# LayerNorm's gain and offset on the residual copy: from GpSimd to VectorE, one quarter in each gate chunk

## What is computed

```python
def layer_norm(x, g, b):
    xf = x.astype(jnp.float32)
    mu = jnp.mean(xf, axis=-1, keepdims=True)
    var = jnp.mean(jnp.square(xf - mu), axis=-1, keepdims=True)
    return ((xf - mu) * lax.rsqrt(var + LN_EPS)).astype(x.dtype) * g + b
...
        x = layer_norm(DEEPNORM_ALPHA * x + y, ln_g[i], ln_b[i])
        x = x + (p[i] @ w_ple[i]) * jax.nn.sigmoid(x @ w_ple_gate[i])
```

## Time and profile before

| | us |
|---|---|
| median of 3 runs | 1190.71 |
| lowest and highest | 1190.23, 1191.17 |
| profiled execution, span from first to last instruction | 1189.1 |
| TensorE busy | 1166.7 |
| VectorE busy | 741.6 |
| ScalarE busy | 589.7 |
| GpSimd busy | 68.4 |

### The profile page before, as it was taken

One profiled execution on the slowest core, in us unless ns is written; L12 is line 12 of the kernel. 1 busy time (PEld: TensorE's weight loads), 2 busy tenths in 40 slices (PEclk: granted clock), 3 DMA queues, 4 the chain that ended last, 5 costly groups with the idle time before them and its releaser, 6 DMA issues.

```text
span 1189.1 us, 15576 instructions
## 1 busy us (share of the span) xinstructions
PE 1166.7 (98%) x5484; PEld 974.4 (82%) x5484; DVE 741.6 (62%) x762; ACT 589.7 (50%) x661; POOL 68.4 (6%) x59
## 2 busy tenths in 40 slices
PE   8999999999999999989999999999999999999898
PEld 7888888888888888768888888888888888887686
DVE  6665556546556565788667665456776666658762
ACT  5665465456447543445444445545554445434541
POOL 1000000000000100530000000000000000007100
PEclk9999999999999999999999999999999999999899
DMA  9855655665565766247655555654545566762671
GB/s 308 273 159 177 178 160 175 185 185 160 173 182 168 253 235 203 95 162 249 224 197 165 189 182 188 187 183 160 177 159 176 159 232 212 234 192 67 202 234 52
DMA packets 112490, 221.50 MB, mean 186 GB/s; under 512 B 6800, under 2 KB 8848, under 8 KB 111936
## 3 DMA queue, kind: packets, MB, share of 16 engines
q1 hardware_dynamic: 109904, 209.74, 55.7%
q0 software_dynamic: 2544, 11.19, 2.7%
HBM read 216.71 MB, written 4.19 MB: 186 GB/s over the span
## 4 chain that ended last, share of the span: by engine, by line
PE 92%; DVE 4%; issue 1%; ACT 1%; DMA 1%; SPq 0%; ACTq 0%; DVEq 0%
PE acc L1040 28%; PE acc L1042 28%; PE acc L1041 28%; PE aux L1065 2%; PE aux L1082 2%; DVE act L684 1%; DVE w_lo L669 1%; DVE stage L853 1%; PE aux L1106 1%; ACT act L432 1%; PE aux L1120 1%; DMA raw<-in_w_ple_gate 0%; PE aux L1269 0%; DMA raw<-in_w_in_a 0%; PE aux L1041 0%
## 5 line engine op out<-in xcount | busy, mean ns | idle before, releaser
L669 DVE TENSOR_TENSOR w_lo<-raw,w_hi 128x1024 fp32r<-128x1024 f32 x392 | 490.1, 1257 | 377.6 <-ACT w_hi L419 376.0
L419 ACT ACTIVATE w_hi<-raw 128x1024 fp32r<-128x1024 f32 x392 | 413.7, 1059 | 477.0 <-PE acc L1042 426.3
L1040 PE MATMUL acc<-w_hi,act 128*128 128x512 f32 x1552 | 613.8, 395 | 15.7 <-DVE act L684 13.3
L1042 PE MATMUL acc<-w_hi,act 128*128 128x512 f32 x1552 | 606.4, 391 | 0.0
L1041 PE MATMUL acc<-w_lo,act 128*128 128x512 f32 x1552 | 605.7, 390 | 0.0
L1040 PEld LDWEIGHTS acc<-w_hi,act 128*128 128x128 f32 x1552 | 292.6, 189 | 75.3 <-DVE act L684 14.6
L1042 PEld LDWEIGHTS acc<-w_hi,act 128*128 128x128 f32 x1552 | 292.3, 188 | 62.4
L1041 PEld LDWEIGHTS acc<-w_lo,act 128*128 128x128 f32 x1552 | 292.8, 189 | 58.2
L432 ACT ACTIVATE act<-stage 128x1024 fp32r<-128x1024 f32 (+1 forms) x12 | 12.7, 1060 | 52.2 <-DVE stage L853 52.2
L684 DVE TENSOR_TENSOR act<-stage,act 128x1024 fp32r<-128x1024 f32 (+1 forms) x12 | 21.3, 1779 | 14.3 <-ACT act L432 14.3
L515 ACT ACTIVATE heads<-aux,neg_max 128x128 f32<-128x128 f32 (+1 forms) x32 | 13.0, 420 | 23.6 <-DVE neg_max L969 23.6
(11 more groups left out here) (144 smaller groups left out, 603.7 us busy)
## 6 DMA issues: line engine op xcount, KB each, us to landing
raw<-in_w_in_a SPq DMA_DIRECT2D x128, 512.0 KB, 3.7
raw<-in_w_ple_gate SPq DMA_DIRECT2D x64, 512.0 KB, 4.9
raw<-in_w_in_b SPq DMA_DIRECT2D x64, 512.0 KB, 3.6
raw<-in_w_kv SPq DMA_DIRECT2D x64, 512.0 KB, 3.6
raw<-in_w_out_a SPq DMA_DIRECT2D x32, 512.0 KB, 4.5
raw<-in_w_out_b SPq DMA_DIRECT2D x32, 512.0 KB, 4.5
heads<-in_ln_rows POOLq DMA_DIRECT2D x4, 1024.0 KB, 8.3
raw<-in_w_ple SPq DMA_DIRECT2D x8, 512.0 KB, 3.8
```

What stands on the lines that cost most here:

```text
L419: nc.scalar.activation(w_hi[:, r], raw[:, r % RAWS], ACT.Copy).then_inc(hi_ready, 1)
L669: nc.vector.tensor_tensor(w_lo[:, r], raw[:, r % RAWS], w_hi[:, r].bitcast(F32), ALU.subtract) \
L1040: nc.tensor.matmul(dst, hi, w_hi[:, r, i], start=begin, stop=False)
L1042: mm = nc.tensor.matmul(dst, lo, w_hi[:, r, i], start=False, stop=end)
```

## The change

The multiply by the gain and the addition of the offset on the residual copy leave GpSimd's queue and enter VectorE's, quarter by quarter: quarter 0 behind the split of index 4 in gate chunk 0, quarters c of the loop behind the split of index 5 of gate chunk c, and in layer 1 quarter 3 ahead of the last gate. They work on the same places with the same shapes. They wait for the rows, for ScalarE's norm of all four quarters, and the add for the multiply; the wait for the transposes is left out, since VectorE's L853 waited for them earlier in the same queue.

```diff
-        gained = sem("pool_gained")
-        x1_ready = sem("pool_x1_ready")
+        gained = sem("dve_gained")
+        x1_ready = sem("dve_x1_ready")
...
-            def gain_and_offset(layer):
-
-                pool.wait_ge(ln_rows_landed, 32 * (layer + 1))
-                for c in range(G):
-                    x1 = columns(res[layer], c)
-                    row = lambda r: r[:, c * COLS:(c + 1) * COLS].unsqueeze(1).broadcast_to((P, TT, COLS))
-                    pool.wait_ge(lnT_psum, (2 * G if layer else 0) + c + 1)
-                    nc.gpsimd.tensor_tensor(x1, x1, row(gain), ALU.mult).then_inc(gained, 1)
-                    pool.wait_ge(gained, layer * G + c + 1)
-                    nc.gpsimd.tensor_tensor(x1, x1, row(offset), ALU.add).then_inc(x1_ready, 1)
...
             inverse_std(0)
-            gain_and_offset(0)
...
             inverse_std(2)
-            gain_and_offset(1)
...
+            def gain_and_offset(layer, c):
+
+                e = c + layer * G
+                x1 = columns(res[layer], c)
+                cols = slice(c * COLS, (c + 1) * COLS) if isinstance(c, int) else bass.ts(c, COLS)
+                row = lambda r: r[:, cols].unsqueeze(1).broadcast_to((P, TT, COLS))
+                dve.wait_ge(ln_rows_landed, 32 * (layer + 1))
+                dve.wait_ge(normed_1, 2 * layer * G + G)
+                nc.vector.tensor_tensor(x1, x1, row(gain), ALU.mult).then_inc(gained, 1)
+                dve.wait_ge(gained, e + 1)
+                nc.vector.tensor_tensor(x1, x1, row(offset), ALU.add).then_inc(x1_ready, 1)
+
...
-                pieces(n, n, {PC - 1: [lambda: add_ple(layer, 0)]}, before={0: turned[3]})
+                pieces(n, n, {4: [lambda: gain_and_offset(layer, 0)], PC - 1: [lambda: add_ple(layer, 0)]},
+                       before={0: turned[3]})
                 with dve.Fori(1, G - layer) as c:
                     pieces(c * PC + n, n, ({3: [lambda: x2_lo(c - 1)]} if layer == 0 else {})
-                           | {PC - 1: [lambda: add_ple(layer, c)]})
+                           | {5: [lambda: gain_and_offset(layer, c)], PC - 1: [lambda: add_ple(layer, c)]})
                 if layer:
                     c = G - 1
+                    gain_and_offset(layer, c)
```

## The result

The changed kernel takes 1172.25 us (median of 4 runs, 1172.12 to 1172.59); the kernel before took 1190.47 us in the same comparison. The ratio is 0.9845, with a 95% interval of 0.9833 to 0.9856. The forecast was 1172.1 us with a range of 1171.0 to 1178.0.

The account below looks back on a forecast made before the run. TensorE, busy 98%, was taken as the bound, held up by VectorE in both norms. Savings of 9.07 (layer 0) and 9.56 us (layer 1) take the span 1189.1 to 1170.5; plus 1.6 gives 1172.1 us, range 1171.0 to 1178.0.

Parts of the forecast that it names:

- GpSimd's turns with VectorE: In both norms, GpSimd's SBUF reads and VectorE's two-input instructions exclude each other: 3.02 and 3.40 us beside 1.23.
- The norm of layer 0: Gate chunk 0 of layer 0: TensorE's waits and slow clock up to piece 6 go, saving 8.75 us.
- layer 1, 9.56: Gate chunk 0 of layer 1: piece 6 starts at 1103.60 in place of 1113.16, saving 9.56 us.
- The layout of VectorE's order: Norm of layer 0 without GpSimd: low halves of quarters 1 to 3 start at 498.76, 505.92 and 512.35.
- the margins for quarters 1 to 3: Layer 0's normed low halves are usable 3.7, 2.1 and 1.2 us before TensorE asks for them.
- The second input: Second layer input of quarter 0, layer 0: TensorE's 0.31 us of lateness goes, with 0.1 us to spare.
- moved with it, it comes 18.64 us behind L684: Layer 0: the second input's transpose keeps its distance from quarter 3's low half and comes at 530.99.
- The cost of the pairs: The 16 operations on VectorE take 1.23 us each, 2.40 us a pair with steps, covered by idle in the gate chunks.
- its 0.45 us: Gate chunk 0 of layer 0: the pair and three splits fit before L870 with 0.45 us to spare.
- Moved, not saved: Rival: VectorE's added 19.8 us lies on the path, giving 1191.9 us, no change; chance 0.04 together with another cause.
- Starving behind the pairs: Rival: TensorE starves at splits behind pairs in seven gate chunks, costing 17 to 34 us, 1189 to 1206; chance 0.04.
- thinner cover: Rival: late loads or ScalarE copies leave TensorE waits at quarters 2, 3 and the second input, 1174 to 1180; chance 0.13.

Follow-up runs that it names:

- Runs 3 and 4: Changed kernel plus GpSimd work at the old place whose result nobody uses: operations that read SBUF, 1191.05 us; then memsets that only write, 1172.0 us.
- run 2: Against the changed kernel: gain and offset on VectorE, but each pair right behind the low half of its quarter, near GpSimd's old place; 1189.79 us.
- runs 1 to 8: All follow-up kernels; 1: GpSimd's old operations delayed to the new places, 1173.0 us; 7: change in layer 0 alone, 1181.40; 8: chunk 0's sigmoid and gated addition one split earlier, 1171.88.
- run 6: Changed kernel with each pair doubled by two more VectorE multiplies of the same size whose result nobody reads; 1174.02 us.
- Run 5: Changed kernel without the gain multiply and offset addition on the residual copy, semaphore waits kept; 1172.44 us.

## Why the prediction was right

The four corners put together, medians in us:

| | beside the norm | in the gate chunks |
|---|---|---|
| GpSimd | 1190.47 | 1173.0 |
| VectorE | 1189.79 | 1172.25 |

**The cause.** I laid the stalls on GpSimd's turns with VectorE. Runs 3 and 4 show that: the stalls need no dependence, and they need GpSimd to read. But the table shows what I did not say: at the old place it hardly matters for the time who does the work. The gain is the place; each engine gets it there.

The two times at the old place are nearly equal by coincidence, for they are made up of different terms. GpSimd held VectorE up for longer: behind the norm's last transposes, the low half of quarter 3 started after 18.55 us in the kernel before (502.99 to 521.54), after 15.83 us in run 2 (502.37 to 518.20) and after 9.36 us in the changed kernel (502.18 to 511.54). So piece 6 came 8.8 us late in layer 0 with GpSimd and 5.3 us late with VectorE's own pairs. Run 2 then loses 3.0 us more up to the second input and 2.6 us to the clock behind it. In layer 1 it loses 7.0 us where the kernel before loses 9.6.

**Term by term.** The norm of layer 0 was to give 8.75 us and gave 20.55 - 11.77 = 8.78; layer 1, 9.56, and 21.36 - 11.80 = 9.56. The layout of VectorE's order met quarters 1 to 3 to 0.01 us, and all of the margins for quarters 1 to 3 held.

**The second input** was to give 0.32 us and cost 0.68 instead: from piece 6 to its transposes TensorE took 17.32 us, where it was 16.64 before and 16.32 would be without a wait. So this term was wrong in its sign, its margin of 0.1 us was lost, and layer 0 gave 37.19 - 29.09 = 8.10 us in all up to these transposes, where 9.07 were forecast. My step was "moved with it, it comes 18.64 us behind L684"; it came 19.73 us behind (511.54 to 531.27). The pair is not the reason, with idle of 0.21 and 1.11 us behind it, both of them waits for ScalarE. The high half of piece 13 waited for its load. ScalarE's timeline in the changed kernel:

```profile
518.10 1.06 ACT L406 ACTIVATE w_hi<-raw 128x1024 fp32r<-128x1024 f32 x1 [2.79 <-DMA raw<-in_w_ple_gate]
521.92 1.06 ACT L406 ACTIVATE w_hi<-raw 128x1024 fp32r<-128x1024 f32 x1 [2.77 <-DMA raw<-in_w_ple_gate]
```

The second of these, for piece 13, is 2.77 us, and was 1.41 before. In the eight experiments it is 1.19, 2.10, 3.29, 1.64, 1.27, 1.60, 2.24 and 1.39 us (runs 1 to 8). In the changed kernel SyncE issued this load at 515.20, 5 us before the pair starts, and with the doubled pair (run 6) the idle is 1.60 us. So the landing varies by up to 2 us between these profiles, one of each kernel; what makes it vary stays open.

**The start.** The sum lacked a term: this profile is 0.81 us early before the first norm. TensorE's first product of weights starts at 8.68 us before and at 7.94 after, but between 8.04 and 8.82 us in the profiles of the eight experiments, in which nothing at the start differs. I take it for chance and not for the change; no run isolates it. The full account of the spans is 8.10 + 9.56 + 0.81 = 18.47 of 18.5 us; that the forecast met the span to 0.1 us owes that much to two misses of opposite sign.

**The cost of the pairs.** 1.22 and 1.23 us were measured for the 1.23 taken. The pair with the step to the next instruction takes 2.39 us where a split follows at once (run 2, 501.69 to 504.08), for the 2.40 taken. Run 5 shows that they cost nothing measurable, run 6 that the cover in chunk 0 ends between one pair and two, as its 0.45 us had said.

**The rivals.** "Moved, not saved" was given 0.04, with the remark that the warning of the Trainium skill (Perfetto Trace Analysis, Optimizing Scalar/DVE Operations) decides only if the place is as tight as the old one. Run 2 is that case, and the warning held there: 1189.79 us. Starving behind the pairs is refuted by runs 5 and 6; thinner cover did not come about, save for the loads' 1 us.

## What to carry to other kernels

Take a stretched instruction as a hint of another engine's reads, as here: the same line with the same shape at 1.23 and at 3.4 us, ending 1.08 us behind GpSimd's instruction. Then ask first whether the other work can go elsewhere in time, and only then to which engine: work off the critical path belongs where the helping engine is idle, and a doubled and an empty version of it tell how much cover there is. To forecast such a change, lay the held engine's queue out from undisturbed durations and compare each step with the time at which the bound engine asks for it.

## What was unexpected of the hardware

The clock's price does not follow from the length of the idle alone. In run 2 TensorE stood idle for 1.79 us ahead of quarter 2 in both layers, 2.18 us between matmul starts. In layer 0 (508.47 to 510.65) steps of 0.43 us followed, from 511.29 to 514.28, at a granted clock of 0.57; in layer 1 (1100.09 to 1102.27) the matmuls went on at full pace. There the 3.04 us ahead of quarter 3 brought the slow steps, up to 1115.3. In the kernel before, the idle of 1.53 us ahead of quarter 1 did nothing, and the 5.08 us ahead of quarter 2 brought 0.53:

```profile
505.55 0.50 PE L1040 MATMUL acc<-w_hi,act 128*128 128x512 f32 x1 [1.53 <-DVE act L684]
```

What decides between two equal idles stays open. In run 2 the slow stretches make the difference of about 4 us between the 14 expected from the waits and the 17.5 measured. And a GpSimd memset of 128x1024 takes 1.01 us (24.28 / 24), where its operations with two inputs take 2.4.
